# Last down stage of a two-pass fp32 encoder layer: order of the last loads, place of one gate form, place of one residual

## The reference, cut to what matters

```python
def conv_ffn(hn, w_ffn_in, conv_w, conv_b, w_ffn_down):
    u, v = jnp.split(hn @ w_ffn_in, 2, axis=-1)          # D_FF = 2816 each
    ...                                                  # uc: width-3 depthwise convolution of u
    return (jax.nn.gelu(uc) * v).astype(dt) @ w_ffn_down
h = h + conv_ffn(rmsnorm(h, norm_ffn[l]), w_ffn_in[l], conv_w[l], conv_b[l], w_ffn_down[l])
return rmsnorm(h, norm_final)
```

## Time and profile before

| | before |
|---|---|
| median of 3 runs | 1246.33 us (1245.38 to 1246.88) |
| profiled execution | 1245.58 us |
| its span | 1243.8 us |
| TensorE busy | 1210.3 us (97%) |
| VectorE busy | 808.4 us (65%) |
| ScalarE busy | 528.4 us (42%) |
| GpSimd busy | 97.3 us (8%) |

### The profile page before, as it was taken

One profiled execution on the slowest core, in us unless ns is written; L12 is line 12 of the kernel. 1 busy time (PEld: TensorE's weight loads), 2 busy tenths in 40 slices (PEclk: granted clock), 3 DMA queues, 4 the chain that ended last, 5 costly groups with the idle time before them and its releaser, 6 DMA issues.

```text
span 1243.8 us, 18442 instructions
## 1 busy us (share of the span) xinstructions
PE 1210.3 (97%) x6989; PEld 1100.5 (88%) x6989; DVE 808.4 (65%) x1217; ACT 528.4 (42%) x832; POOL 97.3 (8%) x109
## 2 busy tenths in 40 slices
PE   6999999999999999999999998999999999999986
PEld 5999899999999998888888888989989989989974
DVE  7594586378359454322323488797896897887787
ACT  5353335145145243222221247544545645536554
POOL 0000000000000000000000121112121111211120
PEclk9999999999999999999999999999999999999999
DMA  4301111211111111222124126555456465465552
GB/s 173 138 35 52 64 37 50 76 37 51 34 63 37 48 52 51 69 68 67 51 67 175 63 64 151 117 124 131 119 124 131 111 144 120 103 149 131 130 97 102
DMA packets 42192, 112.09 MB, mean 90 GB/s; under 512 B 4624, under 2 KB 4880, under 8 KB 42128
## 3 DMA queue, kind: packets, MB, share of 16 engines
q1 hardware_dynamic: 27584, 84.42, 19.8%
q0 software_dynamic: 13968, 25.43, 12.7%
q10 hardware_dynamic: 576, 1.38, 0.3%
HBM read 107.54 MB, written 3.15 MB: 89 GB/s over the span
## 4 chain that ended last, share of the span: by engine, by line
PE 89%; DVE 6%; ACT 1%; DVEq 1%; issue 1%; DMA 1%; SPq 0%; POOL 0%; ACTq 0%
PE ps L1586 45%; PE ps L1829 23%; PE ps L1912 10%; PE ps L1683 3%; PE ps L1623 3%; PE ps L1676 1%; DVE ring L1288 1%; PE ps L1693 1%; PE ps L1611 1%; DVE af L1309 1%; DVE h L1266 1%; PE ps L1613 1%; DMA raw<-in_pairs 0%; DVE gf L1394 0%; PE ps L1568 0%
## 5 line engine op out<-in xcount | busy, mean ns | idle before, releaser
L1586 PE MATMUL ps<-hn,ring 128*128 128x256 f32 (+1 forms) x2544 | 462.6, 337 | 0.3 <-DVE hn L966 0.3
L1586 PEld LDWEIGHTS ps<-hn,ring 128*128 128x128 f32 x2544 | 388.5, 191 | 46.7 <-issue 0.7
L1829 PE MATMUL ps<-af,ring 128*128 128x384 f32 x1848 | 325.3, 335 | 5.5 <-DVE af L1309 3.2
L1829 PEld LDWEIGHTS ps<-af,ring 128*128 128x128 f32 x1848 | 320.3, 188 | 9.7 <-DVE af L1309 4.8
L1912 PE MATMUL ps<-ring,gf 128*128 128x512 f32 x693 | 161.7, 391 | 6.9 <-DVE h L1266 3.9
L1912 PEld LDWEIGHTS ps<-ring,gf 128*128 128x128 f32 x693 | 129.2, 188 | 36.9 <-issue 6.0
L937 DVE TENSOR_TENSOR ring<-raw,ring 128x1024 fp32r<-128x1024 f32 x68 | 83.1, 1224 | 119.2 <-ACT ring L510 114.8
L753 ACT ACTIVATE ring<-raw 128x512 fp32r<-128x512 f32 x164 | 96.7, 622 | 48.8 <-DMA raw<-in_pairs 46.8
L1288 DVE TENSOR_TENSOR ring<-raw,ring 128x512 fp32r<-128x512 f32 x164 | 107.4, 684 | 13.5 <-ACT ring L753 13.2
L559 ACT ACTIVATE sig<-ps 128x768 f32<-128x768 f32 x36 | 29.2, 812 | 179.9 <-PE ps L1586 179.8
L510 ACT ACTIVATE ring<-raw 128x1024 fp32r<-128x1024 f32 x68 | 71.6, 1055 | 28.8 <-PE ps L1586 10.1
(11 more groups left out here) (172 smaller groups left out, 1215.8 us busy)
## 6 DMA issues: line engine op xcount, KB each, us to landing
raw<-in_units SPq DMA_DIRECT2D x68, 512.0 KB, 3.5
raw<-in_pairs SPq DMA_DIRECT2D x33, 512.0 KB, 4.3
raw<-in_pairs SPq DMA_DIRECT2D x66, 256.0 KB, 3.6
raw<-in_pairs POOLq DMA_DIRECT2D x64, 256.0 KB, 4.1
tb<-in_pairs POOLq DMA_DIRECT2D x31, 256.0 KB, 4.5
strips<-in_strips SPq DMA_DIRECT2D x4, 896.0 KB, 4.4
x_in<-in_x_s SPq DMA_DIRECT2D x4, 512.0 KB, 5.4
h<-in_x_s SPq DMA_DIRECT2D x1, 2048.0 KB, 8.1
```

Source lines behind the costliest of these rows:

```text
L1586: ins = pe.matmul(out, w if stationary_w else x, x if stationary_w else w, start=start and i == 0, stop=stop and i == 2)
L1829: ins = pe.matmul(ps[:, bank, 0:HALF], ring[:, p, a, k * P:(k + 1) * P], af[:, x, b, k, :], start=first and k == 0 and j == 0, stop=k == H ...
```

## The change

1. SyncE loads unit 32 ahead of unit 31.
2. The gate form A11 of q = 10 (`gate_hi(20)`, `gate_lo(20)`) is made inside the loop, right after pair 21's third copy and third join, ahead of the pieces of places 350 to 352 and `centre(21)` on ScalarE, and of the pieces of places 349 to 351 and `join_last(21)` on VectorE. ScalarE's wait ahead of every gate form of q = 10 is now product S2(21), where it was S4(21).
3. VectorE makes the low piece of place 354 (S2 of q = 10) ahead of `gate(21)`, where it came with the first of the seven steps' pieces behind it.
4. In the step of S1, VectorE adds S1's residual first, ahead of the pieces of places 360 to 362. The weighing of the first half of tokens 0 to 383, which stood at the end of the step of S2, comes behind these pieces.

```diff
-            for j in SEQ:
+            for j in SEQ[:-2] + [SEQ[-1], SEQ[-2]]:
                 b, prior = raw_of(j), prior_of(j)
...
                     if q == LAST_Q:
 
-                        act.wait_ge(fdone, ORD[NF - 1, S4] + 1)
+                        act.wait_ge(fdone, ORD[NF - 1, S2] + 1)
...
                     hi_upto(PLACE[i, S3] + 6)
-                    if i > lo and i < NF - 1:
+                    if i > lo:
                         gate_hi(i - 1)
...
                 if hi == NF:
-                    gate_hi(NF - 2)
                     hi_upto(PLACE[down_pair(qs[-1]), A11] + 6)
...
-                    if i > lo and i < NF - 1:
+                    if i > lo:
                         gate_lo(i - 1)
...
                 if hi == NF:
-                    gate_lo(NF - 2)
                     conv(hi - 1)
-                    lo_upto(PLACE[down_pair(qs[-1]), A11] + 5)
+                    lo_upto(PLACE[down_pair(qs[-1]), A11] + 6)
                     gate(NF - 1)
...
                 for n, x in enumerate(DOWN[d]):
+                    if hi == NF and n == 3:
+                        down_sums(d, hi, qs, x, range(3))
                     if hi < NF or n < 6:
                         lo_upto(PLACE[down_pair(qs[-1]), x] + 5)
...
-                    if 0 < n < 6:
+                    if 0 < n < 6 and n != 3:
                         down_sums(d, hi, qs, x, range(3))
-                    if n == 2:
+                    if n == 3:
                         dve.wait_ge(fin_ld, 16)
                         for t in range(3):
                             dve.tensor_tensor(hw[:, t, early(t)], h[:, t, early(t)], wfin[:, early(t)], ALU.mult).then_inc(weighed, 1)
-                    elif n == 3:
                         dve.wait_ge(half_sq, 3)
```

## The result

| | before | after |
|---|---|---|
| median | 1246.33 us (1245.38 to 1246.88, 6 runs) | 1237.77 us (1237.62 to 1239.08, 6 runs) |
| profiled execution, its span | 1245.58, 1243.8 us | 1237.86, 1236.1 us |

The ratio is 0.9936, 95% interval 0.9926 to 0.9946: faster by more than the 0.2% that can be told. The medians differ by 8.56 us, the spans by 7.7. The differences of 2 us and less that follow are read from the profiles; the medians alone tell few of them apart.

The account below looks back on a forecast made before the run. TensorE, busy 97%, gains only at holes or behind its last matmul; the end is VectorE's. The S4 residual moves from 1221.33 to 1214.95, 6.4 us, its 22.5 us chain unchanged: 1246.33 - 6.4 = 1239.9 us; range 1238.0 to 1242.4.

Parts of the forecast that it names:

- What bounds the kernel: Last 70 us: TensorE has five holes, 7.58 us together, from unit 32's late loads; VectorE's fixed 22.5 us sets the end.
- the first rival: After S1, VectorE's pieces overlap more, TensorE sets the end: S4 residual at 1213.6, gain 7.7 us, 1238.6; chance 0.17.
- The loads: SyncE issues unit 32's loads at about 1166.6; GpSimd makes 32's sum at about 1171.7, 31's at 1176.7; loss taken as 0.
- First holes, gate: At pair 21, TensorE's first two holes go; convolution at 1185.9, gate at 1190.7, 4.75 us earlier.
- Slack at S1: Before S1(8), VectorE writes the A12 residual's first third at 1201.4, TensorE wants it at 1202.1: smallest slack, 0.7 us.
- The residual of S1: Put ahead of the weighing, it starts at 1207.3 after VectorE stands 1 us; worth 1.0 us, removing a 2.96 us hole.
- VectorE's lateness: At the S4 residual, VectorE comes at 1214.95, TensorE has S4 ready at 1213.5: 1.4 us late.
- The old order: With weighing first, at the new times, the S1 residual would start at 1210.1 and the S4 residual at about 1215.9.
- The last chain: VectorE from S4 residual to end: residual, weighing, root, S3 residual, three A22 rounds; fixed at 22.5 us, keeps its length.
- The second: A wait replaces the removed ones, at 31's sum or S1: 1 to 2.5 us lost, 1241 to 1242.3; chance 0.22.
- the fourth: Unit 32's loads collide with A22(21)'s landing sum, TensorE waits at A22(21) or S3(21), kernel slower; chance 0.03.
- The third: Loads not early enough, 32's sum still at 1183, only the S1 residual's place helps: gain 1.6 us, 1244.7; chance 0.04.

Follow-up runs that it names:

- all but loads: The changed kernel with SyncE's load order taken back, unit 31 again ahead of unit 32: median 1243.23 us, ratio 0.9974 (0.9965 to 0.9984).

## Why the prediction was right, and where not

**What bounds the kernel:** right on all three engines, wrong in one sentence. The clock "stays at its upper level across the longest of them, so a hole costs its length and nothing on top" was read off one execution that happened to have no fall, in a window that ends ahead of the matmuls behind the longest hole. A second execution of the same kernel has two, one of which cost 1.3 us, and four versions with holes of 1.9 us and more each have one of about 1.6. This is the step that failed. It touches the median, not the profile: no profile of the changed kernel or of a version that keeps all of its parts, or lacks one of the two small ones, has a fall in this stage. The falls are a part of what the 8.56 us of the medians have over the 7.21 of the stage. Beside its time, the mean granted clock of the whole execution is on record for 36 timed executions of the kernel before. It was 0.998 in the profile without a fall and 0.993 in the one with two. The four executions at 0.998 average 1245.7 us, the eight at 0.993 1246.9, and all 36 average 1246.3. By that the falls make about 0.6 of the 1.35 us, as an estimate, for such a mean does not say where the clock fell. The first 30 us add a scatter of their own (A11(8) began between 1177.65 and 1179.29 us in the profiles of all versions).

**The number and the mechanism.** The measured median is nearest to that of the first rival (1238.6), and the S4 residual even began at the rival's 1213.6. Both are chance: TensorE had the product 1.5 us earlier, VectorE stood nowhere ahead of it, and the stage as a whole began 0.5 us earlier. The forecast named the right mechanism and was 0.8 us too small for the stage (6.4 for 7.21).

**The loads:** right. Issued 1166.1 (forecast 1166.6), 32's sum 1172.0 (1171.7), 31's 1175.4 (1176.7), no stand at `sum_three(31)`. Alone they are worth 4.7 us of the stretch with the clock set apart, though the holes that they removed on TensorE's timeline, 1.67, 1.95 and 0.16 of the 0.76 us, add up to 3.8; of the rest, 0.42 is a wait that the timeline does not show (below).

**First holes, gate:** right. The convolution began at 1185.31 and the gate at 1189.99, 6.94 and 11.62 us after A11(8); forecast 7.0 and 11.8.

**Slack at S1:** the right place with the wrong size. S1(8) began 1201.43 - 1200.59 = 0.84 us behind the start of the A12 residual in the version without the gate form, where it waited for it. In the changed kernel that residual began at 1200.02, which allows 1200.86, and TensorE came at 1184.64 + 72 x 0.227 = 1201.0 (0.227 is found below): a slack of 0.1 us, not 0.7. So most of the 0.6 us by which VectorE was later without the gate form turned into loss.

**The residual of S1:** the right mechanism with a mis-sized term. The S1 residual began 27.61 us after A11(8), forecast 28.4. The stride of 0.234 us was too long: it was (12.81 - 0.39)/53 over a row that the earlier trace rows shows as whole, and that holds a wait. TensorE's weight loads, in the timeline of the kernel before, show it:

```profile
1191.24 6.01 PEld L1912 LDWEIGHTS ps<-ring,gf 128*128 128x128 f32 x27 [2.36 <-issue]
1197.66 5.99 PEld L1912 LDWEIGHTS ps<-ring,gf 128*128 128x128 f32 x27 [0.42 <-issue]
```

The 0.42 us lie where A12(10) begins, whose gate form VectorE started at 1196.99 (L1394). Without them it is 0.227, as in the changed kernel: (34.91 - 0.39)/152. Over 93 matmuls that is 0.65 of the 0.8 us by which the forecast missed. VectorE stood 0.31 us ahead of the residual, not 1.0. From there to the S4 residual the forecast was 7.65 us; it is 7.63. VectorE's lateness was 1.5 us (forecast 1.4): 1205.98 + 27 x 0.227 = 1212.1, against 1213.61. By the versions without this part, it is worth 36.85 - 35.24 = 1.6 us with the clock up (forecast 1.0), and 3.3 with a fall (38.58). The old order was forecast rightly (1215.9 - 1178.88 = 37.0 for 36.85), as VectorE's own queue sets it; the stride error lies in the new order alone, where the S1 residual waits for TensorE.

**The last chain** kept its 22.5 us. **Rivals:** the first did not come, VectorE stayed late. The second and the fourth did not either: no sum was late, and no hole opened before A22. The third is near to "all but loads", where the loads stay late and 2.9 us remain with the clock set apart; it had 1.6, reckoned without the other two parts.

## What to carry to other kernels

Where two engines keep hand-written orders over the same transfers, lay the orders side by side: here one queue that takes 32 before 31, behind another that loads 31 first, cost 4.7 us, and it shows as long idle time on the engine nobody looks at. Take strides from rows that are checked for hidden waits (the weight loads show them, the matmuls do not), and a hole of 2 to 3 us on TensorE, as here, at more than its length, unless several executions show the clock up. Work moved to an idle engine is not free: GpSimd's weighing cost VectorE 2.4 us where it took 1.8 off it.

## What the runs showed of the hardware

- In the last stage the clock fell behind holes of 1.76, 1.91, 2.33, 2.94, 2.95 and 2.96 us, and did not behind others of like length (1.67, 1.95 and 2.96 in the first profile of before, 1.75 after, 1.72 and 1.71 with weighings on GpSimd). Over all profiles, it fell behind none of ten holes of 1.65 to 1.75 us and behind six of eight of 1.76 to 2.96, too few to name a limit. A fall cost TensorE about 1.6 us each time: 54 matmuls of 512 columns in 14.10 to 14.15 us for 12.5, 24 of 384 in 6.00 for 4.43.
- With fourteen useless matmuls in such a hole the clock stood at 1.00 in the one profile taken, and the stretch was 1.7 us shorter than in the profile with the hole.
- GpSimd's multiplication of 128x512 beside VectorE's pieces took 1.57 us each (4.70 for three) and made three pieces 4.29 us for 1.88; three residuals that read PSUM, two of them beside it, kept their 1.89.
- A table load of 1.28 us on ScalarE could be moved forward by a one-column root: squares and copies did not load another table afterwards, and the S3 residual came 0.45 us earlier.
